# In each attention stage three of the streamed adaptive units are weighted and summed on VectorE instead of TensorE

## What is computed

```python
# first block, for l in range(2):
shift, scale, gate = jnp.split(c @ w_ada[l] + b_ada[l], 3, axis=-1)      # c is (1, 1024), w_ada[l] is (1024, 3072)
u = x * (1.0 + scale) + shift
...                                                                       # projections, three kinds of attention
x = layer_norm(ALPHA * x + (1.0 + gate) * y, ln_g[l], ln_b[l])
# second block
mod   = jax.nn.silu(c_2)   @ w_mod + b_mod                                # w_mod is (1024, 6144)
mod_c = jax.nn.silu(c_ctx) @ w_mod + b_mod
sh1, sc1, gt1, sh2, sc2, gt2 = jnp.split(mod, 6, axis=-1)                 # of mod_c only the first two parts are used
```

## Time and profile before

| | us |
|---|---|
| median of 3 runs | 1246.29 |
| lowest and highest | 1242.06, 1248.05 |
| the profiled execution's own time | 1242.05 |
| its span (first to last instruction) | 1240.2 |
| TensorE busy in the span | 1062.4 (86%) |
| VectorE busy | 433.0 (35%) |
| ScalarE busy | 236.2 (19%) |
| bytes moved by DMA | 323.66 MB, mean 261 GB/s |

### The profile page before, as it was taken

How to read it: one execution, slowest core, us unless ns; L and a number is a source line. 1 busy time by engine, 2 the same in 40 slices (tenths; PEclk the granted TensorE clock), 3 DMA queues, 4 the chain that set the end, 5 groups by cost and what they waited for, 6 DMA issues and landing times.

```text
span 1240.2 us, 17860 instructions
## 1 busy us (share of the span) xinstructions
PE 1062.4 (86%) x7574; PEld 574.9 (46%) x7574; DVE 433.0 (35%) x1026; ACT 236.2 (19%) x584; POOL 54.3 (4%) x69
## 2 busy tenths in 40 slices
PE   5899999999999999999998989898767667666676
PEld 2344764444476447985667975442211112111111
DVE  0138636333764527345246764511000001000001
ACT  0012135011213513344112341210000000000002
POOL 0101000000100000000222310000000000000000
PEclk9999989999999999899998999899978887888876
DMA  9963328443336974013231014999999999999995
GB/s 385 396 254 136 128 88 336 173 176 136 136 115 239 429 303 153 1 68 143 73 126 69 4 43 163 365 394 429 429 428 433 430 427 433 429 429 429 431 430 250
DMA packets 28014, 323.66 MB, mean 261 GB/s; under 512 B 3248, under 2 KB 3376, under 8 KB 5792
## 3 DMA queue, kind: packets, MB, share of 16 engines
q1 hardware_dynamic: 25904, 314.18, 62.0%
q0 software_dynamic: 2032, 8.35, 1.9%
HBM read 321.47 MB, written 1.05 MB: 260 GB/s over the span
## 4 chain that ended last, share of the span: by engine, by line
PE 59%; DMA 29%; DVE 7%; issue 3%; ACT 1%; SPq 0%; POOL 0%; DVEq 0%; ACTq 0%; POOLq 0%
PE banks L640 47%; DMA zuv_to_Kt<-in_stream 16%; DMA ring<-in_stream 7%; DMA Vt_to_O<-in_stream 3%; DMA scr_qk<-in_stream 3%; PE banks L651 3%; PE banks L2167 1%; PE banks L901 1%; PE banks L887 1%; PE banks L922 1%; PE banks L884 1%; PE banks L788 1%; DVE probs L1245 1%; PE banks L892 0%; DVE KC L1237 0%
## 5 line engine op out<-in xcount | busy, mean ns | idle before, releaser
L640 PE MATMUL banks<-ring,uT 128*128 128x512 f32 (+1 forms) x512 | 222.8, 589 | 7.9 <-DMA ring<-in_stream 4.0
L640 PEld LDWEIGHTS banks<-ring,uT 128*128 128x128 f32 x512 | 95.3, 190 | 120.0 <-issue 112.0
L640 PE MATMUL banks<-scr_qk 64*64 64x64 f32 (+4 forms) x2368 | 115.5, 275 | 12.4 <-DMA scr_qk<-in_stream 7.5
L640 PE MATMUL banks<-ring,scr_qk 128*32 128x512 f32 (+1 forms) x496 | 91.2, 699 | 34.8 <-DMA ring<-in_stream 34.4
L640 PEld LDWEIGHTS banks<-scr_qk 64*64 64x64 f32 (+3 forms) x2368 | 85.1, 138 | 42.5 <-issue 24.4
L2677 DVE SCALAR_TENSOR_TENSOR UWK<-UWK,banks 128x256 f32<-128x256 f32 x16 | 6.7, 421 | 270.9 <-ACT UWK L2944 270.9
L640 PE MATMUL banks<-ring,UWK 128*32 128x512 f32 (+1 forms) x336 | 83.7, 758 | 15.0 <-ACT UWK L2952 9.2
L2944 ACT ACTIVATE UWK<-banks 128x256 f32<-128x256 f32 x16 | 6.1, 383 | 363.2 <-PE banks L640 363.2
L640 PE MATMUL banks<-UWK,ring 128*128 128x256 f32 x320 | 72.4, 386 | 0.0
L640 PEld LDWEIGHTS banks<-ring,scr_qk 128*32 128x32 f32 (+1 forms) x496 | 25.2, 130 | 91.9 <-DMA ring<-in_stream 50.8
L640 PEld LDWEIGHTS banks<-UWK,ring 128*128 128x128 f32 x320 | 61.9, 194 | 9.5 <-issue 1.0
(11 more groups left out here) (374 smaller groups left out, 1222.4 us busy)
## 6 DMA issues: line engine op xcount, KB each, us to landing
ring<-in_stream SPq DMA_DIRECT2D x94, 2048.0 KB, 13.8
scr_qk<-in_stream SPq DMA_DIRECT2D x11, 2048.0 KB, 38.8
Vt_to_O<-in_stream SPq DMA_DIRECT2D x11, 2048.0 KB, 39.3
zuv_to_Kt<-in_stream SPq DMA_DIRECT2D x10, 2048.0 KB, 38.8
scr_qk<-in_stream SPq DMA_DIRECT2D x11, 1024.0 KB, 40.2
wide<-in_stream SPq DMA_DIRECT2D x10, 1024.0 KB, 38.2
const<-in_stream SPq DMA_DIRECT2D x10, 1024.0 KB, 37.8
misc<-in_stream SPq DMA_DIRECT2D x10, 1024.0 KB, 40.0
```

Of the source, the lines that this page charges most:

```text
L640: return pe.matmul(o, a, b, start=start, stop=stop)
```

## The change

Of the 6 units of `w_ada[1]`, numbers 0, 1 and 2, and of the 12 of `w_mod`, numbers 8, 9 and 10, go to VectorE. It multiplies each chunk of 128x512 with the vector's value of that partition and adds it up in an SBUF tile `acc` (which lies on `w1`): one `tensor_scalar` and seven `scalar_tensor_tensor` for a unit, 24 instructions in a stage, spread over steps 2 to 10 behind `v_probT` as 2, 3, 3, 2, 3, 3, 2, 3, 3. A unit's event is now signalled behind its eighth instruction. TensorE keeps the other units (in layer 0 in steps 3, 6 and 9; in layer 1 one in each of the steps 2 to 10), and at the start of step 11 it adds the partitions of the three `acc` rows with a window that holds a column of ones (`pe_parts`, 3 matmuls of 32x512). The rows are read out behind that. The order of the units in the stream changes with it: each vector unit comes ahead of the TensorE units of the same third.

```diff
+BY_VECTOR = {0: (0, 1, 2), 1: (8, 9, 10)}
...
         if l + 1 < DEPTH:
-            for cg in range(6):
+            for cg in (0, 3, 1, 4, 2, 5):
                 cols("w_ada", l + 1, cg * 512, 512, "ada_mm", l + 1, cg)
         else:
-            for cg in range(12):
+            for cg in (8, 0, 1, 2, 9, 3, 4, 5, 10, 6, 7, 11):
                 cols("w_mod_2", 0, cg * 512, 512, "mod_mm", cg)
...
+        acc = w1[:, :, :, :].rearrange("p v a n -> p (v a n)").rearrange("p (i n) -> p i n", i=4)
...
                 pool.wait_ge(*at("cmp1", l - 1, 1))
+                pool.wait_ge(*at("part_mm", l - 1))
             pool.dma_start(w1[:, :, :, :], A["w1"][l].rearrange("p (v a n) -> p v a n", v=2, a=LPAIR)).then_inc(*tick("cmp_in", by=16))
...
+        def pe_parts(pe, l):
+
+            for j, n in enumerate(BY_VECTOR[l]):
+                pe.wait_ge(*at(*unit_event(l, n)))
+                r = 31 - (2 * n if l else n)
+                ins = pe.matmul(bank[7][32 * j:32 * j + 32, :], onewin[:, r:r + 32], acc[:, j, :], start=False, stop=True)
+            ins.then_inc(*tick("bank7_filled", "part_mm", l))
...
                 if 2 <= m < NPAIR:
                     if l + 1 < DEPTH:
-                        for n in range(6 * (m - 2) // 9, 6 * (m - 1) // 9):
-                            pe_ada(pe, l + 1, n)
+                        if m in (3, 6, 9):
+                            pe_ada(pe, l + 1, 2 + m // 3)
                     else:
-                        for n in range(12 * (m - 2) // 9, 12 * (m - 1) // 9):
-                            pe_mod_rows(pe, n)
+                        pe_mod_rows(pe, m - 2 if m < 10 else 11)
                 if m == NPAIR:
+                    pe_parts(pe, l)
                     w_out += [take(pe)]
                     pe_y(pe, l, 0, 0, w_out, range(0, 5))
...
+            dve.memset(onewin, 0.0).then_inc(*tick("vector_step"))
...
+            dve.memset(onewin[:, 31:32], 1.0).then_inc(*tick("vector_step"))
...
-            dve.wait_ge(*at("ada_mm", l, 5 if l else 2 + half))
+            dve.wait_ge(*(at("part_mm", 0) if l else at("ada_mm", 0, 2 + half)))
...
+        def v_unit_rows(dve, l, part):
+
+            win, col = (modwin, MOD_AT) if l else (adawin, ADA_AT)
+            for s in part:
+                i, k = s // DCH, s % DCH
+                n = BY_VECTOR[l][i]
+                w, o, c = take(dve, k=units.index(unit_event(l, n))), acc[:, i, :], win[:, k, col:col + 1]
+                if k == 0:
+                    ins = dve.tensor_scalar(o, w[:, k, :], c, None, ALU.mult)
+                else:
+                    dve.wait_ge(*last("vector_step"))
+                    ins = dve.scalar_tensor_tensor(o, w[:, k, :], c, o, ALU.mult, ALU.add)
...
                 if 0 <= m - 2 < NPAIR:
                     v_probT(dve, l, m - 2)
+                if 2 <= m < NPAIR:
+                    every = len(BY_VECTOR[l]) * DCH
+                    v_unit_rows(dve, l, range(every * (m - 2) // 9, every * (m - 1) // 9))
...
-            dve.wait_ge(*at("mod_mm", 11))
+            dve.wait_ge(*at("part_mm", 1))
```

More of the change, by code:

```diff
@@ L144, in constants, with by_vector @@
     return c
+BY_VECTOR = {0: (0, 1, 2), 1: (8, 9, 10)}
+def by_vector(*event):
+    return (event[0:2] == ("ada_mm", 1) and event[2] in BY_VECTOR[0]) or (event[0] == "mod_mm" and event[1] in BY_VECTOR[1])
 def unit_order():
@@ L347, in build @@
         adawin = kc_flat[:, 512:512 + DCH * (ADA_AT + 32)].rearrange("p (k n) -> p k n", k=DCH)
+        onewin = kc_flat[:, 944:944 + 63]
         modwin = kc_flat[:, 512:512 + DCH * (MOD_AT + 32)].rearrange("p (k n) -> p k n", k=DCH)
@@ L502, in build, with take @@
         unit_at = [0]
-        def take(pe, n=512):
-            k = unit_at[0]
-            unit_at[0] += 1
+        def take(pe, n=512, k=None):
+            if k is None:
+                while by_vector(*units[unit_at[0]]):
+                    unit_at[0] += 1
+                k = unit_at[0]
+                unit_at[0] += 1
             pe.wait_ge(K.sem(f"arrived{slot[k]}"), 16 * use[k])
@@ L640, in mm, with pe_rows @@
             return pe.matmul(o, a, b, start=start, stop=stop)
-        def pe_rows(pe, event, window, at_col, step, n, first, final, b):
+        def pe_rows(pe, event, window, at_col, step, n, first, final, b, kept=0):
             w = take(pe)
@@ L652, in pe_rows @@
                                     w[:, j * (DCH // 4) + k, :], start=(n, k) == (first, 0),
-                                    stop=(n, k) == (final, DCH // 4 - 1))
+                                    stop=(n, k) == (final, DCH // 4 - 1) and j >= kept)
             if n == first:
@@ L663, in pe_ada @@
             else:
-                first, final, b = 0, 5, 7
-            pe_rows(pe, ("ada_mm", l), adawin, ADA_AT, 1, n, first, final, b)
+                first, final, b = 3, 5, 7
+            pe_rows(pe, ("ada_mm", l), adawin, ADA_AT, 1, n, first, final, b, 3 if l else 0)
         def pe_mod_rows(pe, n):
-            pe_rows(pe, ("mod_mm",), modwin, MOD_AT, 2, n, 0, 11, 7)
+            pe_rows(pe, ("mod_mm",), modwin, MOD_AT, 2, n, 0, 11, 7, 3)
+        def pe_parts(pe, l):
[4 more added lines that the diff above has]
+            ins.then_inc(*tick("bank7_filled", "part_mm", l))
+            K.events["use", "part_mm", l] = K.events["use", "mod_mm", 0] if l else K.events["use", "ada_mm", 1, 3]
         def pe_ada_columns(pe, l, half=0):
@@ L1410, in v_gT, with unit_event @@
             dve.scalar_tensor_tensor(g, g, 1.0, bank[b], ALU.add, ALU.mult).then_inc(*drain(b, "gT", l, i))
+        def unit_event(l, n):
+            return ("mod_mm", n) if l else ("ada_mm", 1, n)
+        def v_unit_rows(dve, l, part):
[7 more added lines that the diff above has]
+                else:
+                    dve.wait_ge(*last("vector_step"))
+                    ins = dve.scalar_tensor_tensor(o, w[:, k, :], c, o, ALU.mult, ALU.add)
+                if k < DCH - 1:
+                    ins.then_inc(*tick("vector_step"))
+                else:
+                    ins.then_inc(*tick("vector_step", *unit_event(l, n)))
         def v_attend(dve, l):
```

## The result

The changed kernel takes 1297.05 us as a median of 4 runs (1291.16 to 1299.93), the kernel before 1244.76 in 4 runs: a ratio of 1.0423, with the 95% interval 1.0384 to 1.0462. It is 52 us slower. The prediction had 1281 and the range 1264 to 1298, so the sign and the place were right and the size was 16 us short; the measured median lies 1 us inside the upper end of the range. The profiled execution of the changed kernel took 1291.16 us, its span is 1289.3: 49.1 more than the span of before.

What follows compares the result with a forecast made beforehand. Bound: a full-rate expert-weight stream at the end, nothing before it having slack, layer 1's attention stage transfer-bound, layer 0's TensorE-bound. Layer 0 6.7 + layer 1 25.2 + clock 4 = 35.9 on 1242.05: 1278, median 1281, range 1264 to 1298.

Steps and rivals of the forecast that it cites:

- What layer 0 or layer 1 loses is lost at the end, one for one: Whole kernel: nothing between the early layers and the final full-rate expert-weight stream has slack to absorb a delay.
- the queue catches up: Rival, layer 1: only one gap up to 406.1, then a full queue; `w_out` +10.7, total 1264; chance 0.12.
- not slower: Rival, both stages: VectorE's additions fit into its idle time; median 1242, within 0.5%; chance 0.04.
- the loads share the rate: Rival, layer 1: four loads issued together land together, each group costing the chain 10 us; about 1306; chance 0.06.
- The term of 25.2: Layer 1's attention stage: held slots and in-order issue make `w_out` land at 466.1 against 440.91, +25.2 us.
- after 6.5 us: Layer 1's stream: a unit issued into an idle queue lands 6.5 us after its issue.
- Chained instructions at 0.73: VectorE, both stages: each `scalar_tensor_tensor` takes 0.73 us to its successor's start; 24 instructions make 16.9 us.
- 0.7 a wait: TensorE's clock: each wait ahead of a unit costs 0.7 us of slow clock, priced at one lengthened step.
- predicted 6.7: Layer 0's attention stage: +4.5 us from step 4 to step 10's copy, +2.2 in step 11, together +6.7.
- The stretch from the projection of layer 1 to the end as long as before: Rest of the program behind layer 1's attention stage: claimed unchanged in length.
- the clock's 4: TensorE after its new waits: lower granted clock costs +4 us, taken between 2.8 and 8.6.
- layer 0's 3.2 + 2.2: Layer 0's lower bound: +3.2 us up to step 10's copy with all waits hidden, +2.2 in step 11.

Runs made afterwards that it cites:

- layer0_only: Changed kernel with VectorE units in layer 0 only, layer 1 as in the kernel before: 1255.96 us, ratio 1.0112 to the kernel before.
- layer1_only: Changed kernel with VectorE units in layer 1 only, layer 0 as in the kernel before: 1286.56 us, ratio 1.0348 to the kernel before.
- order_only: Kernel before with only layer 1's new unit order in the stream and on TensorE, which does all twelve units: 1240.05 us, ratio 0.9978.
- hold_only: order_only plus slots of units 8, 9, 10 given back only by tiny VectorE memsets in steps 4, 7, 10: 1274.51 us, 1.0261 to the kernel before.
- work_only: Layer 0 as before; layer 1 has VectorE's 24 instructions, but each unit's first frees its slot, the others read a constant: 1255.98 us, ratio 1.0122.
- immediate: Changed kernel with the constant 1.0 instead of the vector's value from SBUF in chained instructions: 1289.23 us, ratio 1.0397 to the kernel before.
- one_unit: Kernel before with only layer 0's unit 5 on VectorE, layer 1 as before: 1242.76 us, ratio 1.0004.
- filled_half: Changed kernel with constant TensorE matmuls filling layer 1's waits, 13 ahead of units 3 and 6, 5 ahead of `w_out`: 1288.16 us, ratio 1.0373.
- nine_later: Layer 0 as before; layer 1 has only units 8 and 9 on VectorE, unit 9 behind unit 5 in the stream: 1250.20 us, ratio 1.0074.

## Why the prediction was right, and where it was short

**The bound.** "What layer 0 or layer 1 loses is lost at the end, one for one": right. The first transfer that the chain has behind layer 1's projection starts 51.7 us later (931.72 against 880.02), and the full stretch goes on from there at the same 430 GB/s; 2.6 us come back in it. layer0_only and layer1_only add up. One reading was off without harm: the full stretch doesn't begin at about 745 us but at about 775, as the slice from 744 to 775 us has a DMA digit of 4.

**Layer 1: the mechanism.** Right in each part: the fifth issue waits for VectorE's eighth instruction, three more stand behind it with free slots, TensorE waits in steps 5 and 8 and for `w_out`. order_only, hold_only and work_only take it apart, and hold_only shows that the slots alone give most of it (25.7 of 35.9 us in the stage). The rivals "the queue catches up" (stage 1 +10.7) and "not slower" fall with the DMA share of 0.61 and the three groups of issues; "the loads share the rate" falls with `w_out`: it was the first of four loads issued together and landed after 7.7 us, while the second of the other two groups came after 12.6.

**Layer 1: the size.** The term of 25.2 measured 35.9. Piece by piece, predicted and measured, from step 2's scores on:

| piece | predicted | measured |
|---|---|---|
| to unit 8 done | 17.7 | 18.2 |
| unit 3 landed behind the issue | 11.4 | 12.7 |
| from there to unit 9 done | 15.2 | 19.1 |
| unit 6 landed | 11.4 | 12.6 |
| from there to unit 10 done | 15.5 | 18.1 |
| `w_out` landed | 6.5 | 7.7 |

The steps that were mis-sized:
- The landing into an idle queue, "after 6.5 us": 7.7, three times 1.2 us, 3.7 in all. I had it as the remainder of a sum over ten units and 1 MB of context rows. That sum was wrong: the context rows had been issued at 372.40 and had landed 5.7 us later, and the DMA engines moved nothing from 380 to 388 us. Without them the remainder is 4.0 and the landing would have been put at 8.9. No sum was needed, as the trace of before has just such a load, the one issued at 388.12 (its issue, KB, us to landing):

```profile
ring<-in_stream SPq DMA_DIRECT2D x1, 2048.0 KB, 7.7
```

- Chained instructions at 0.73: the rows have 0.75 for one and 2.46 for three, which is 0.85 to 0.86 from start to start. Of the 0.12 too little, 0.06 are the value read from SBUF (immediate: 0.69 for one). The other 0.06 are a longer gap: 0.10 to 0.11 us between two instructions here and in immediate, where each waits for two events, the landing of its unit and its predecessor, and 0.04 in work_only, where a chained one waits for the predecessor alone and reads a constant in place of the chunk, so that three take 2.32:

```profile
397.09 2.32 DVE L1458 SCALAR_TENSOR_TENSOR w<-const,KC,w 128x512 f32<-128x512 f32 x3
```

  So it isn't the wait for the predecessor; that it is the second wait and not the other operand is likely, not shown. In all this makes about 2.4 us over the stage, small against the rest.
- The clock. Behind each wait of 13.8 us the unit takes 3.64 us (1.92 at full clock) and the transposes 1.54 (0.87): 2.4 us, twice. I had priced 0.7 a wait, from a row behind a short wait; the ends of the range named the half clock only for the projection. Measured: about 4.7 in the stage, 1.4 in the projection, and, less surely, the 5 us below: 11 in place of 4. The Trainium skill's TensorE: Matmul & The Clock Gate (HAM oscillation), which makes a low stretch cost half its length, had given some 2 us a wait; these rows agree with that better than with the step of the earlier trace rows by which I went: from 426.12 to 431.17 us the granted clock is 0.50 for 5.05 us, and the same work took 2.66 before, 2.4 less.

**Layer 0.** The end of the stage came 6.9 us later, predicted 6.7, but that is luck: the stage is 9.0 longer, less the 2.1 us by which it started earlier. (The same code took 47.2 to 49.5 us in five profiles, so some 2 us of it vary.) The steps up to the copy cost 6.5 instead of 4.5, the end 2.5 instead of 2.2. I had VectorE as the bound from step 4 on, with 1 us of waiting, in step 6. From the maxima of step 4 (184.16) to the end of the copy of step 10 (220.62) it waited twice, 1.96 us in step 6 and 2.04 in step 9, which has a unit of TensorE too and which I had left out. The other 32.5 of the 36.5 us are what I had put for its work and gaps (20.8 + 11.3 + 0.4). Ahead of each of these two waits the chain of waits leaves VectorE and passes through the other two engines: late maxima, then the exponentials of ScalarE, and behind them, in ScalarE's order, its half of the copy of probabilities, for which TensorE waits.

```profile
206.90 0.61 DVE mx L1401
...
207.53 0.47 ACT probs L1655 x2
...
208.02 0.92 ACT probs L1655 x4
...
209.53 0.39 ACT H L1667
...
209.96 1.09 PE banks L945 x4
211.05 0.43 PE banks L948 x4
211.48 2.84 PE banks L665 x16
214.32 0.82 PE banks L924 x6
```

I had followed only VectorE's copy (`v_probT`) there, which stands ahead of the new instructions and so is not delayed by those of its own step. Behind TensorE's waits of 1.77 us in step 6 and 2.46 in step 9 comes the low clock, in layer 0 too; the units there take 2.80 and 2.91 us in place of 1.92. The one of step 9:

```profile
209.96 1.09 PE L945 MATMUL banks<-H 128*64 128x256 f32 x4 [2.46 <-ACT H L1667]
...
211.41 2.91 PE L665 MATMUL banks<-ring,KC 128*32 128x512 f32 x16
```

The same path is seen at the end of one_unit's stage. The end of the stage, 3.40 us from the copy to the projection as against 3.2, was right, and inside too. TensorE does wait for ScalarE's copy until 221.50, but this is hidden: the third matmul of `pe_parts` starts only at 223.04, when the last of VectorE's three instructions is done, and takes 1.0.

```profile
220.54 2.45 DVE L1456 SCALAR_TENSOR_TENSOR w<-ring,KC,w 128x512 f32<-128x512 f32 x3
223.04 0.14 PEld L689 LDWEIGHTS banks<-w,KC 128*32 128x32 f32 x2 [0.60 <-DVE w L1456]
```

**The rest.** "The stretch from the projection of layer 1 to the end as long as before" was wrong by 6.4 us. 1.4 are the slow projection; another 7.6 are lost up to the first transfer of the chain, and 2.6 come back in the full stream. Those 7.6, 5 on balance, lie in the second block, in its sequential parts, where the granted clock is lower, as in this table of the same piece of work (before it took 64.07 us at 0.95):

```profile
548.91:616.26 67.35, 65.18 (x310) 57.34 (x310) 28.30 (x72) 27.09 (x62) 0.00 (x0) 0.90 0.14 47
```

In the profiled executions the kernels that touch layer 1 with held slots or VectorE's work all have 804.6 to 813.5 from the projection on; before, order_only, layer0_only and one_unit have 794.2 to 800.9. The four kernels named last already differ by 6.7 us among themselves, though the code from the projection on is the same. So it seems to go with the change and not with chance, but why is open: filled_half, with the waits mostly filled, kept it (805.7). That a stage changes the granted clock of work a hundred microseconds later is argued from single profiles, not shown.

With the 4.2 us by which I had set the median over the profiled execution the forecast stood at 1281; the changed kernel's median is 5.9 over its profile. Of the 16 us missing, 10.7 are stage 1 and 6.4 the rest, less the clock's 4 that I had added; the remainder is the median's 1.7 and a slip in my addition, as 1242.05 + 35.9 + 4.2 is 1282. Nor does the lower end of the forecast's own range, 1268, follow from its terms: layer 0's 3.2 + 2.2, layer 1's 25.2 and the cheap clock's 2.8 give 1280. The upper end, 1296, lay below the result, which the full range, ending at 1298, holds by 1 us.

## What to carry to other kernels

In a ring that one engine issues in order, the price of a consumer is above all how long it holds its slot, not how long it works: three slots kept to the place of VectorE's eighth instruction cost the stage 26 us with none of the work done, while the work without the hold cost it 5. If a load has to go to a slower consumer, place it in the stream so that its slot is asked for only when it is done (nine_later: 1.8 us in the stage, though 8.0 in the median). Follow every engine whose queue passes the new instructions to its next consumer, two engines on as well. A wait costs TensorE its length and then the slow clock behind it; price that from the row behind the longest wait to be found. And before working out how long a load takes to land, look for one in the trace that met the same queue.

## What the runs showed of the hardware

- A load of 2.097 MB into an idle queue landed 7.7 us after its issue, before (388.12) and in the changed kernel, and the second of a group 12.6 to 12.7 after the first one's issue; in a full queue they come 4.85 us apart.
- Three chained `scalar_tensor_tensor` of 128x512 in fp32, all in SBUF, took 2.46 us with the scalar read from SBUF and 2.28 with a constant (0.75 and 0.69 for one). The gap between two of them was 0.10 to 0.11 us where each waited for two events and 0.04 where it waited for one.
- Behind a wait of 13.8 us the same unit took 3.64 us instead of 1.92, and behind 11.43 us of filling and a rest of 2.3 us 1.92; but behind the same filling and 2.6 us, 3.49. The granted clock isn't settled by the last wait alone.
- An fp32 matmul of 128x512 is two records and 0.87 to 0.88 us at full clock (22.58 for 26, 11.43 for 13), twice what I had taken for one.
